# An encoder with eight experts: the whole down projection split, weights in 2 MB slabs, a short piece requested later

## The chip, the cores and the metric

The kernel runs on one core of a Trainium2 chip. Its time is the device time of one execution in microseconds (us); the times given are medians over runs on one chip. A profiled execution is one such run with the hardware profiler on.

## The reference, cut to what matters

Two batches of 256 tokens pass through two layers that share their weights. The change lies in the last block of the second layer, where each token goes through two of eight experts:

```python
def swiglu(x, w_g, w_u, w_d):
    return (jax.nn.silu(x @ w_g) * (x @ w_u)) @ w_d

def moe_swiglu(x, w_router, b_router, w_g, w_u, w_d):
    logits = (x @ w_router).astype(jnp.float32) + b_router.astype(jnp.float32)
    top_v, top_i = lax.top_k(logits, TOP_K)          # TOP_K = 2
    top_w = jax.nn.softmax(top_v, axis=-1)
    ...
    for e in range(N_EXPERTS):                        # 8
        y = y + combine[..., e:e + 1] * swiglu(x, w_g[e], w_u[e], w_d[e])
    return y
```

The width is 1024 (8 tiles of 128), an expert's hidden width 1408 (11 tiles). All is float32.

## The kernel before, in words

The attention, pooling, convolution and dense blocks run first and take until about 1040 us; the change does not touch their work. Then a router sorts the 512 tokens, twice each, into **items**: 128 rows that belong to one expert. Here there are 11 items. Their number is read from a table on the chip, so each engine's program has a first item (SP and VectorE), a loop, and a final item.

**Pieces.** The weights of an item come in 17 pieces (`PIECES`, line 74). Pieces 0 to 9 hold two feature blocks of gate and up weights, four of the eight contraction tiles each; piece 10 holds the last feature tile with all eight. Pieces 11, 12 and 13 are the first half of the output columns of the down projection, with contraction tiles 0 to 3, 4 to 7 and 8 to 10; pieces 14, 15 and 16 are the same for the second half. Pieces 13 and 16, with three contraction tiles, are the short ones: 128 partitions by 1536 numbers, where the others have 2048.

**Split products.** A float32 product is made from three fast ones: a matrix is split into a high part in the format fp32r and a low part, the rest. ScalarE writes the high part of a weight piece (`e_split`, lines 740 to 749), VectorE the low part (`e_low`, 1099 to 1105), and TensorE multiplies high by high, high by low and low by high (lines 1749 to 1751). The short pieces are not split: TensorE multiplies them as plain fp32 (line 1757), which the trace shows as two instructions per matmul. So the transposed hidden features are split for tiles 0 to 7 only (`hidden_high` 787, `hidden_low` 1215) and kept whole for tiles 8 to 10.

**Slots.** Fifteen pieces of an item pass through a ring of eight landing slots of 1 MB, six in `eraw` and two in `erawx`; the short pieces have two places of their own, `eplain`. Split parts lie in a ring of three (`ESPL`). SP requests the pieces in order (`expert_piece`, lines 469 to 483, waiting in `slot_free`, 485 to 502): a slot is free when VectorE has written the low part of what it held, a place of `eplain` when TensorE has used it. In the loop (515 to 523) SP requests pieces 3 to 16 of an item and then 0 to 2 of the next. A piece's rows are 2 KB long in memory, those of a short one 1.5 KB.

**The order of work** is written out by hand for each engine. TensorE (lines 1761 to 1780) takes pieces 0 to 16, transposes the hidden features of a block in between (1728), and turns the next item's rows into features behind piece 12 (1699). ScalarE (809 to 830) splits three pieces ahead of TensorE, with the tanh of each block, the high parts of the features, the load of the next item's rows behind piece 5's split (`load_rows`, 760), the next item's features (`xg_high`, 766 to 778) and the copies of the results (`y_out`, 795) in between. VectorE (1236 to 1254) follows with the low parts and the gating of the hidden rows; in the first item it also scales the residual (`residual_base`, 1193), in the last it adds gathered results into `X` (`add_rest`, 1268).

The lines that say how the last stretch of an item is ordered on ScalarE are:

```python
hidden_high(4, j)
e_split(14, j)            # the 15th split piece: piece 15
hidden_high(5, j)
e_split(0, j + 1)
xg_high(j + 1)
y_out(0, j)
e_split(1, j + 1)
e_split(2, j + 1)
y_out(1, j)
```

Of the kernel before, what the change touches and what calls it, by code (L numbers as in the profile page):

```python
# [34 lines left out]
P = 128  # L35
# [41 lines left out]
F_SPLIT = 8  # L77
SPLIT = [p for p in range(NPC) if p not in (13, 16)]
NSP = len(SPLIT)
RAWP = [p for p in range(NPC) if p not in SPLIT]  # L80
ERING, EMAIN, ESPL = 8, 6, 3
EW = 2048
N_BLK = 6
LOADS = [len([o for o in range(NSP) if o % ERING == s]) for s in range(ERING)]
# [3 lines left out]
C_COS, C_SIN, C_INV = 640, 896, 1152  # L88
C_I8, C_I16 = 1664, 1672
C_TOK = 1688  # L90
C_END = 1692
# [51 lines left out]
def build_trunk(nc, x0, x1, dense_w, expert_gu, expert_dn, consts, slots, vecs, mix, lnrow, wr, br, xd, yd, y0, y1):  # L143
    ctx = ExitStack()
    with ctx:
# [16 lines left out]

        cst = at("cst", [P, C_END], F32)
        vec = at("vec", [P, DEPTH, V_END], F32)
        hvec = at("hvec", [P, DEPTH, 32], F32)
        mixw = at("mixw", [P, DEPTH, 2, P], F32)
# [67 lines left out]
        eraw = at("eraw", [P, EMAIN, EW], F32)  # L234
# [10 lines left out]
        eplain = at("eplain", [P, 2, EW], F32, o)  # L245
        erawx = at("erawx", [P, ERING - EMAIN, EW], F32, o + 2 * EW * 4)
# [47 lines left out]
        hth = at("hth", [P, F_SPLIT, CAP], F32R)  # L294
        htl = at("htl", [P, F_SPLIT, CAP], F32R)
        ht32 = at("ht32", [P, FET - F_SPLIT, CAP], F32)
# [61 lines left out]
        in_plain = [sem(f"in_plain{i}") for i in range(2)]  # L358
# [26 lines left out]
        def landed(o, j):  # L385

            return j * (16 * LOADS[o % ERING]) + 16 * (o // ERING + 1)

        def raw_slot(o):

            s = o % ERING
            return eraw[:, s] if s < EMAIN else erawx[:, s - EMAIN]
# [45 lines left out]
        def _(sp):  # L438
# [30 lines left out]
            def expert_piece(e, p):  # L469
                what, b, k0, kn = PIECES[p]  # L470
                if what == "gu":
                    n = 2 * blk(b)
                    src = expert_gu[bass.ds(e * (2 * FET) + 4 * b, n), :, k0 * P:(k0 + kn) * P]
                else:
                    n = 4
                    src = expert_dn[bass.ds(e * KD + 4 * b, n), :, k0 * P:(k0 + kn) * P]
                if p in SPLIT:
                    o = SPLIT.index(p)
                    dst, arrived = raw_slot(o), in_e[o % ERING]
                else:  # L480
                    dst, arrived = eplain[:, RAWP.index(p)], in_plain[RAWP.index(p)]
                dst = dst[:, 0:n * kn * P].rearrange("p (c n) -> p c n", c=n)
                sp.dma_start(dst, src.rearrange("c p n -> p c n")).then_inc(arrived, 16)

            def slot_free(p, j, before=None):

                before = j - 1 if before is None else before
                if p not in SPLIT:
                    if isinstance(j, int) and j == 0:
                        sp.wait_ge(sel_mm, 2)  # L490
                    else:
                        sp.wait_ge(e_used, before * NPC + (p + 1))
                    return
                o = SPLIT.index(p)
                if o >= ERING:
                    sp.wait_ge(e_lo, j * NSP + (o - ERING + 1))
                elif isinstance(j, int) and j == 0:
                    if o >= EMAIN:
                        sp.wait_ge(sel_mm, 2)
                else:  # L500
                    last = max(q for q in range(NSP) if q % ERING == o)
                    sp.wait_ge(e_lo, before * NSP + (last + 1))

            for p in range(NPC):
                slot_free(p, 0)
                expert_piece(0, p)
                if p == EMAIN - 1:
# [4 lines left out]
            for p in range(ESPL):  # L512
                slot_free(p, 1)
                expert_piece(e, p)
            with sp.Fori(1, final) as j:

                e = sp.value_load(tab[0:1, bass.ds(j, 1)], min_val=0, max_val=NE - 1)
                for p in range(ESPL, NPC):
                    slot_free(p, j)
                    expert_piece(e, p)  # L520
                e = sp.value_load(tab[0:1, bass.ds(j + 1, 1)], min_val=0, max_val=NE - 1)
                for p in range(ESPL):
                    slot_free(p, j + 1)
                    expert_piece(e, p)
            e = sp.value_load(tab[0:1, bass.ds(final, 1)], min_val=0, max_val=NE - 1)
            before = sp.value_load(tab[0:1, 18:19], min_val=NE - 2, max_val=MAX_ITEMS - 2)
            for p in range(ESPL, NPC):
                slot_free(p, final, before)
                expert_piece(e, p)
# [14 lines left out]
        def _(act):  # L544
# [195 lines left out]
            def e_split(o, j):  # L740

                p = SPLIT[o]
                act.wait_ge(in_e[o % ERING], landed(o, j))
                if o >= ESPL:
                    act.wait_ge(e_used, j * NPC + (SPLIT[o - ESPL] + 1))
                elif not isinstance(j, int):
                    act.wait_ge(e_used, (j - 1) * NPC + (SPLIT[o - ESPL] + 1))
                n = (2 * blk(PIECES[p][1]) if PIECES[p][0] == "gu" else 4) * PIECES[p][3] * P
                nc.scalar.activation(ewhi[:, o % ESPL, 0:n], raw_slot(o)[:, 0:n], ACT.Copy).then_inc(e_hi, 1)  # L749
# [37 lines left out]
            def hidden_high(b, j):  # L787
# [3 lines left out]
                dst = hth[:, 2 * b:2 * b + n, :] if 2 * b < F_SPLIT else ht32[:, 2 * b - F_SPLIT:2 * b - F_SPLIT + n, :]  # L791
                nc.scalar.activation(dst, bank[B_HT[b % 2]][:, 0:n * CAP].rearrange("p (a n) -> p a n", a=n),
# [16 lines left out]
            with act.Fori(0, final) as j:  # L809
                for p in range(N_GUP):  # L810
                    if p % 2 == 1 or p == 10:
                        hidden_tanh(p // 2, j)
                    if p == 3:
# [5 lines left out]
                    e_split(p + ESPL, j)  # L819
# [11 lines left out]
            for p in range(N_GUP):  # L831
# [4 lines left out]
                e_split(p + ESPL, final)  # L836
# [9 lines left out]
            act.wait_ge(e_lo, final * NSP + ERING)  # L846
# [25 lines left out]
        def _(dve):  # L872
# [226 lines left out]
            def e_low(o, j):  # L1099

                p = SPLIT[o]
                n = (2 * blk(PIECES[p][1]) if PIECES[p][0] == "gu" else 4) * PIECES[p][3] * P
                dve.wait_ge(e_hi, j * NSP + (o + 1))
                V.tensor_tensor(ewlo[:, o % ESPL, 0:n], raw_slot(o)[:, 0:n], ewhi[:, o % ESPL, 0:n],  # L1104
                                ALU.subtract).then_inc(e_lo, 1)
# [109 lines left out]
            def hidden_low(b, j):  # L1215

                dve.wait_ge(ht_hi, j * N_BLK + (b + 1))
                V.tensor_tensor(htl[:, 2 * b:2 * b + 2, :],
                                bank[B_HT[b % 2]][:, 0:2 * CAP].rearrange("p (a n) -> p a n", a=2),
                                hth[:, 2 * b:2 * b + 2, :], ALU.subtract).then_inc(ht_lo, 1)  # L1220
# [15 lines left out]
            def item(j, first=False):  # L1236

                for p in range(N_GUP):
# [4 lines left out]
                    e_low(p + ESPL, j)  # L1243
# [33 lines left out]
            for p in range(N_GUP):  # L1277
# [4 lines left out]
                e_low(p + ESPL, final)  # L1282
                if p >= 5:
                    add_rest(p - 5)
            e_low(14, final)
            add_rest(6)
# [156 lines left out]
        def _(pe):  # L1443
# [269 lines left out]
            def item(j, more):  # L1713
# [7 lines left out]
                def hidden_features(b):  # L1721

                    pe.wait_ge(e_h, j * N_BLK + (b + 1))
                    if b >= 2:
                        pe.wait_ge(ht_hi, j * N_BLK + (b - 1))
                        pe.wait_ge(ht_lo, j * (F_SPLIT // 2) + (b - 1))
# [139 lines left out]
```

## Time and profile before

| what | value |
|---|---|
| median of 3 runs (lowest, highest) | 1646.91 us (1645.08, 1647.98) |
| profiled execution, its own time | 1647.25 us |
| its span | 1645.4 us |
| TensorE, VectorE, ScalarE, GpSimd busy | 1584.4, 1151.2, 807.4, 170.1 us |
| mean granted clock of TensorE | 0.988 of full speed |
| moved between memory and chip | 324.52 MB |

The span runs from the first to the last instruction of the profiled execution; 1.85 us of its time lie outside. A row of a timeline is one instruction (or a run of equal ones) with its start and duration. In the chain of waits every moment belongs to the one piece of work that the end waited for. "L749" is line 749. A matmul's busy time overlaps the next one's, since matmuls are pipelined; their pace is seen from start to start. Times on the axis count from the start of the span, so 1262 lies in the expert stage.

### The profile page before, as it was taken

Reading aid. Unit: us, or ns where it says so; the run is one execution under the profiler, and the core shown is the slowest. Engines: PE = TensorE matmul, PEld = TensorE weight load, DVE = VectorE, ACT = ScalarE, POOL = GpSimd, SP = SyncE. Lnnn points to the kernel's source line nnn. Section 1 sums busy time; section 2 is a strip of 40 time slices with the busy share of each in tenths; the row PEclk is TensorE's granted clock in tenths of the full one; section 3 lists DMA queues with packets and bytes.
Section 4 is the critical chain, followed back from the end, with each engine's and each line's share of the span. In section 5 each row is a group of like instructions: output and inputs, shape, how many; then the busy total and the mean of one; then the engine's idle time right before and its main releaser. Section 6 shows DMA issues by size and latency. Waiting matters only on the chain.

```text
span 1645.4 us, 20013 instructions
## 1 busy us (share of the span) xinstructions
PE 1584.4 (96%) x7315; PEld 1264.9 (77%) x7315; DVE 1151.2 (70%) x1339; ACT 807.4 (49%) x1095; POOL 170.1 (10%) x112
## 2 busy tenths in 40 slices
PE   7999999999999999999999999789999999999993
PEld 7877777888888888888777778567777777777772
DVE  6888846584434333288888574789888888888886
ACT  5344442252322222253444422557777777777763
POOL 0410005142000000004100051100000000000030
PEclk9999999999999999999999999899999999999997
DMA  5222222325454332212222235199999999999993
GB/s 211 77 91 76 77 102 90 103 76 202 145 201 144 102 122 96 101 66 77 100 67 77 77 115 206 64 397 392 384 372 381 370 371 372 375 372 381 375 337 142
DMA packets 133521, 324.52 MB, mean 197 GB/s; under 512 B 8188, under 2 KB 19836, under 8 KB 132944
## 3 DMA queue, kind: packets, MB, share of 16 engines
q1 hardware_dynamic: 124432, 290.27, 49.5%
q0 software_dynamic: 5872, 21.84, 3.5%
q10 hardware_dynamic: 3152, 11.54, 1.8%
q8 instruction: 42, 0.69, 0.2%
q14 instruction: 23, 0.19, 0.0%
HBM read 297.06 MB, written 27.26 MB: 197 GB/s over the span
## 4 chain that ended last, share of the span: by engine, by line
PE 91%; DVE 4%; issue 2%; ACT 1%; DMA 1%; POOL 1%; ACTq 0%; SPq 0%; DVEq 0%; POOLq 0%
PE bank L1464 15%; PE bank L1465 15%; PE bank L1466 15%; PE bank L1749 8%; PE bank L1751 8%; PE bank L1750 8%; PE bank L1503 4%; PE bank L1504 4%; PE bank L1502 4%; PE bank L1757 3%; PE bank L1728 1%; DVE ewlo L1104 1%; PE bank L1576 1%; PE bank L1589 1%; PE bank L1561 1%
## 5 line engine op out<-in xcount | busy, mean ns | idle before, releaser
L880 DVE TENSOR_TENSOR wlo<-raw,whi 128x1024 fp32r<-128x1024 f32 x170 | 238.9, 1408 | 207.7 <-ACT whi L554 207.4
L1464 PE MATMUL bank<-xth,whi 128*128 128x512 f32 (+1 forms) x976 | 381.5, 391 | 1.7 <-DVE wlo L880 1.7
L1465 PE MATMUL bank<-xtl,whi 128*128 128x512 f32 (+1 forms) x976 | 370.9, 380 | 0.0
L1466 PE MATMUL bank<-xth,wlo 128*128 128x512 f32 (+1 forms) x976 | 370.6, 380 | 0.0
L1104 DVE TENSOR_TENSOR ewlo<-eraw,ewhi 128x2048 fp32r<-128x2048 f32 x132 | 302.0, 2289 | 62.5 <-ACT ewhi L749 62.5
L749 ACT ACTIVATE ewhi<-eraw 128x2048 fp32r<-128x2048 f32 x132 | 252.2, 1911 | 42.8 <-PE bank L1751 42.8
L554 ACT ACTIVATE whi<-raw 128x1024 fp32r<-128x1024 f32 x170 | 178.5, 1051 | 137.0 <-PE bank L1504 123.9
L1464 PEld LDWEIGHTS bank<-xth,whi 128*128 128x128 f32 x976 | 184.3, 189 | 50.5 <-issue 8.5
L1465 PEld LDWEIGHTS bank<-xtl,whi 128*128 128x128 f32 x976 | 184.3, 189 | 36.8 <-issue 3.8
L1466 PEld LDWEIGHTS bank<-xth,wlo 128*128 128x128 f32 x976 | 184.1, 189 | 35.2
L1749 PE MATMUL bank<-ewhi,xgh 128*128 128x512 f32 (+1 forms) x528 | 205.9, 390 | 4.6 <-DVE xgl L1190 2.8
L1751 PE MATMUL bank<-ewhi,xgl 128*128 128x512 f32 (+1 forms) x528 | 197.7, 374 | 0.0
L1750 PE MATMUL bank<-ewlo,xgh 128*128 128x512 f32 (+1 forms) x528 | 197.2, 374 | 0.0
L1749 PEld LDWEIGHTS bank<-ewhi,xgh 128*128 128x128 f32 x528 | 100.2, 190 | 23.4 <-DVE ewlo L1104 4.3
L1750 PEld LDWEIGHTS bank<-ewlo,xgh 128*128 128x128 f32 x528 | 100.4, 190 | 18.7 <-issue 2.4
L1751 PEld LDWEIGHTS bank<-ewhi,xgl 128*128 128x128 f32 x528 | 100.0, 189 | 18.3
L614 ACT ACTIVATE gates<-bank,hvec 128x512 f32<-128x512 f32 x48 | 33.0, 688 | 126.2 <-PE bank L1466 126.2
L968 DVE SCALAR_TENSOR_TENSOR cv<-hpad,vec,cv 128x512 f32<-128x512 f32 x120 | 89.9, 750 | 3.1
L1104 DVE TENSOR_TENSOR ewlo<-erawx,ewhi 128x2048 fp32r<-128x2048 f32 x33 | 75.6, 2292 | 7.9 <-ACT ewhi L749 6.7
L1749 PE MATMUL bank<-ewhi,hth 128*128 128x512 f32 x176 | 75.5, 429 | 0.0
L749 ACT ACTIVATE ewhi<-erawx 128x2048 fp32r<-128x2048 f32 x33 | 63.2, 1916 | 16.2 <-PE bank L1751 14.2
L1751 PE MATMUL bank<-ewhi,htl 128*128 128x512 f32 x176 | 69.0, 392 | 0.0
(280 smaller groups left out, 2229.2 us busy)
## 6 DMA issues: line engine op xcount, KB each, us to landing
eraw<-expert_gu SPq DMA_DIRECT2D x99, 1024.0 KB, 8.2
raw<-dense_w SPq DMA_DIRECT2D x170, 512.0 KB, 3.5
eraw<-expert_dn SPq DMA_DIRECT2D x33, 1024.0 KB, 8.0
erawx<-expert_gu SPq DMA_DIRECT2D x22, 1024.0 KB, 8.2
eplain<-expert_dn SPq DMA_DIRECT2D x22, 768.0 KB, 10.1
erawx<-expert_dn SPq DMA_DIRECT2D x11, 1024.0 KB, 9.1
item_rows<-zero POOLq DMA_DIRECT2D x8, 1024.0 KB, 4.8
rows<-item_rows ACTq DMA_DIRECT2D x10, 512.0 KB, 7.1
```

The costliest lines, as they stand in the source:

```text
L554: nc.scalar.activation(whi[:, g % SPL, :], raw[:, g % RAW, :], ACT.Copy).then_inc(hi_done, 1)
L749: nc.scalar.activation(ewhi[:, o % ESPL, 0:n], raw_slot(o)[:, 0:n], ACT.Copy).then_inc(e_hi, 1)
L880: V.tensor_tensor(wlo[:, g % SPL, :], raw[:, g % RAW, :], whi[:, g % SPL, :], ALU.subtract).then_inc(lo_done, 1)
L968: ins = V.scalar_tensor_tensor(acc, src, w, acc, ALU.mult, ALU.add)
L1104: V.tensor_tensor(ewlo[:, o % ESPL, 0:n], raw_slot(o)[:, 0:n], ewhi[:, o % ESPL, 0:n], ALU.subtract).then_inc(e_lo, 1)
L1464: mm(out, wh, xh, start=first, stop=False)
L1465: mm(out, wh, xl, start=False, stop=False)
L1466: return mm(out, wl, xh, start=False, stop=last)
L1502: mm(out, ah[:, k, t], wh, start=(k == 0), stop=False)
L1749: mm(out, ah[:, k, :], wh, start=(k == 0), stop=False)
L1750: mm(out, ah[:, k, :], wl, start=False, stop=False)
L1751: ins = mm(out, al[:, k, :], wh, start=False, stop=(k == last - 1))
```

## The change

All eleven contraction tiles of the down projection are now split: pieces 13 and 16 get high and low parts like the others, in two places `eshi` and `eslo` of their own, and are multiplied with three fp32r matmuls per tile. The split features grow to eleven tiles. The ring has four slots of 2 MB: one request brings a slab of two pieces (pieces 0 and 1, 2 and 3, and so on; piece 10 alone; 11 and 12; 14 and 15) with rows of 4 KB, and a slot is free when the low parts of both its pieces are written. The two short pieces, called "a" and "b" in the list of requests, share one landing place, `eland`, which lies over constants that are no longer needed. "a" is requested between slabs 6 and 7; "b" once the low part of piece 13 is written, behind slabs 0 to 2 of the next item. The orders of ScalarE and VectorE follow, and the next item's rows are loaded behind piece 8's split.

The diff, cut to its core:

```diff
+SHORT = [13, 16]
+RING = [p for p in range(NPC) if p not in SHORT]
+ERING, EMAIN, ESPL = 4, 3, 3
+SLABS = [("gu", b, 4 if b < 5 else 2) for b in range(6)] + [("dn", h, 4) for h in range(2)]
+LOAD = [0, 1, 2, 3, 4, 5, 6, "a", 7]
+AHEAD = 3
...
+SLAB_END = [max(p for p in RING if slab_of(p) == i) for i in range(NSL)]
...
+        eland = at("eland", [P, 1536], F32, o_cst + 4 * C_COS)
...
+        eraw = at("eraw", [P, EMAIN, 2 * EW], F32)
...
-        eplain = at("eplain", [P, 2, EW], F32, o)
+        eshi = at("eshi", [P, 1536], F32R, o)
+        eslo = at("eslo", [P, 1536], F32R, o + EW * 4)
...
+            def slot_free(i, j, before=None):
...
+                if i == "a":
+                    if not isinstance(j, int):
+                        sp.wait_ge(e_lo, before * NPC + (SHORT[1] + 1))
+                elif i == "b":
+                    sp.wait_ge(e_lo, j * NPC + (SHORT[0] + 1))
+                elif i >= ERING:
+                    sp.wait_ge(e_lo, j * NPC + (SLAB_END[i - ERING] + 1))
...
+                    sp.wait_ge(e_lo, before * NPC + (SLAB_END[i - ERING] + 1))
...
             with sp.Fori(1, final) as j:
...
-                for p in range(ESPL, NPC):
-                    slot_free(p, j)
-                    expert_piece(e, p)
-                e = sp.value_load(tab[0:1, bass.ds(j + 1, 1)], min_val=0, max_val=NE - 1)
-                for p in range(ESPL):
-                    slot_free(p, j + 1)
-                    expert_piece(e, p)
+                following = sp.value_load(tab[0:1, bass.ds(j + 1, 1)], min_val=0, max_val=NE - 1)
+                for i in LOAD[AHEAD:]:
+                    slot_free(i, j)
+                    expert_load(e, i)
+                for i in LOAD[:AHEAD]:
+                    slot_free(i, j + 1)
+                    expert_load(following, i)
+                slot_free("b", j)
+                expert_load(e, "b")
...
-            for p in range(ESPL, NPC):
-                slot_free(p, final, before)
-                expert_piece(e, p)
+            for i in LOAD[AHEAD:] + ["b"]:
+                slot_free(i, final, before)
+                expert_load(e, i)
...
+                if p in SHORT:
+                    act.wait_ge(in_short, j * 32 + 16 * (SHORT.index(p) + 1))
+                    if p == SHORT[1]:
+                        act.wait_ge(e_used, j * NPC + (SHORT[0] + 1))
...
-                    if p == 3:
+                    if p == 6:
                         act.wait_ge(scattered, 16 * 2 * TT)
                         load_rows(j + 1)
...
                 e_split(14, j)
                 hidden_high(5, j)
+                e_split(15, j)
+                xg_high(j + 1)
+                e_split(16, j)
+                y_out(0, j)
                 e_split(0, j + 1)
-                xg_high(j + 1)
-                y_out(0, j)
                 e_split(1, j + 1)
...
+                hidden_low(4, j)
                 e_low(14, j)
+                hidden_low(5, j)
                 if first:
                     for i in range(5, 8):
                         residual_base(i)
                     last_slots()
+                e_low(15, j)
+                xg_low(j + 1)
+                e_low(16, j)
                 e_low(0, j + 1)
-                xg_low(j + 1)
...
-                pe.wait_ge(ht_hi, j * N_BLK + 6)
+                pe.wait_ge(ht_lo, j * N_BLK + 6)
                 piece(13)
```

In the new code `e_split(p)` and `e_low(p)` count pieces; before they counted split pieces only, so that `e_split(14)` was piece 15.

## Rows read from the trace of the kernel before

**Rows 1.** Stretches, 1260 to 1310: us, engines' busy us, clock, DMA share, GB/s

```profile
1260.00:1310.00 50.00, 50.00 (x228) 39.02 (x227) 41.28 (x35) 37.53 (x41) 0.00 (x0) 1.00 1.02 370
```

**Rows 2.** Chain of waits, 1250 to 1350: start us, us, engine, line

```profile
by line: PE bank L1751 28.2%; PE bank L1749 28.1%; PE bank L1750 28.1%; PE bank L1757 10.3%; PE bank L1728 3.6%; PE bank L1699 1.7%
...
1262.19 2.58 PE bank L1757 x6
...
1310.45 0.87 PE bank L1699 x8
1311.32 2.58 PE bank L1757 x6
1314.13 0.23 PE bank L1750
...
1319.35 2.58 PE bank L1757 x6
```

**Rows 3.** Waits, all engines 1060 to 1646, then SP's own 1100 to 1600

```profile
ACT ewhi L749 <- PE bank L1751: 57.0, 43, 6.5
...
SPq L483 <- DVE ewlo L1104: 365.7, 138, 5.8
```

**Rows 4.** Stretches, while the first 1 MB pieces land

```profile
1015.00:1020.00 5.00, 5.00 (x24) 4.14 (x23) 4.97 (x9) 0.62 (x2) 0.00 (x0) 1.00 1.05 387
```

**Rows 5.** Groups by line, 1030 to 1646: busy us, mean ns, idle before

```profile
L1104 DVE TENSOR_TENSOR ewlo<-eraw,ewhi 128x2048 fp32r<-128x2048 f32 x132 | 302.0, 2289 | 62.5 <-ACT ewhi L749 62.5
L749 ACT ACTIVATE ewhi<-eraw 128x2048 fp32r<-128x2048 f32 x132 | 252.2, 1911 | 42.8 <-PE bank L1751 42.8
...
L1218 DVE TENSOR_TENSOR htl<-bank,hth 128x256 fp32r<-128x256 f32 x44 | 18.4, 418 | 0.0
```

**Rows 6.** Timeline of VectorE, end of item 0: start us, us

```profile
1120.79 2.29 DVE L1104 TENSOR_TENSOR ewlo<-eraw,ewhi 128x2048 fp32r<-128x2048 f32 x1
1122.99 1.29 DVE L1190 TENSOR_TENSOR xgl<-xg,xgh 128x512 fp32r<-128x512 f32 x2
```

**Rows 7.** Chain of waits, end of item 0

```profile
1122.84 2.58 PE bank L1757 x6
```

**Rows 8.** Chain of waits, end of the last item

```profile
1612.37 1.29 DVE X L1274
1613.68 1.30 DVE X L1274
1615.00 2.61 DMA item_rows<-X
```

**Rows 9.** DMA, 6 to 16 us, where loads have 4 KB rows

```profile
DMA packets 1293, 4.12 MB, mean 412 GB/s; under 512 B 205, under 2 KB 333, under 8 KB 1293
```

**Rows 10.** DMA requests, 400 to 700: KB each, median us to landing

```profile
raw<-dense_w SPq DMA_DIRECT2D x55, 512.0 KB, 3.5
```

**Rows 11.** Timeline of VectorE, item 4: start us, us, line

```profile
1283.47 2.29 DVE L1104 TENSOR_TENSOR ewlo<-eraw,ewhi 128x2048 fp32r<-128x2048 f32 x1 [0.31 <-ACT ewhi L749]
...
1295.21 2.29 DVE L1104 TENSOR_TENSOR ewlo<-eraw,ewhi 128x2048 fp32r<-128x2048 f32 x1 [0.29 <-ACT ewhi L749]
```

**Rows 12.** Timeline of ScalarE, item 4

```profile
1290.12 1.91 ACT L749 ACTIVATE ewhi<-eraw 128x2048 fp32r<-128x2048 f32 x1
...
1293.26 1.91 ACT L749 ACTIVATE ewhi<-eraw 128x2048 fp32r<-128x2048 f32 x1
...
1316.42 0.58 ACT L800 ACTIVATE yrows<-bank 128x512 f32<-128x512 f32 x1
```

**Rows 13.** Stretches around gaps of TensorE (column three is its busy time)

```profile
339.00:342.00 3.00, 0.61 (x5) 0.37 (x4) 2.19 (x7) 2.97 (x7) 0.00 (x0) 0.98 0.00 0
342.00:345.30 3.30, 3.30 (x17) 3.30 (x17) 3.20 (x11) 3.16 (x8) 0.00 (x0) 0.50 0.02 5
...
1593.00:1595.20 2.20, 0.19 (x2) 0.06 (x1) 2.17 (x5) 0.00 (x0) 1.54 (x2) 1.00 1.05 374
```

More of the change, by code:

```diff
@@ L76, with slab_of @@
 NPC = len(PIECES)
[L77 to L81, printed above, removed]
+SHORT = [13, 16]
+RING = [p for p in range(NPC) if p not in SHORT]
+ERING, EMAIN, ESPL = 4, 3, 3
 EW = 2048
 N_BLK = 6
-LOADS = [len([o for o in range(NSP) if o % ERING == s]) for s in range(ERING)]
+SLABS = [("gu", b, 4 if b < 5 else 2) for b in range(6)] + [("dn", h, 4) for h in range(2)]
+NSL = len(SLABS)
+LOAD = [0, 1, 2, 3, 4, 5, 6, "a", 7]
+AHEAD = 3
+def slab_of(p):
+    what, b, k0, kn = PIECES[p]
+    return b if what == "gu" else 6 + b
+SLAB_END = [max(p for p in RING if slab_of(p) == i) for i in range(NSL)]
 C_ID, C_BLK, C_MEAN, C_ONE, C_TRI = 0, 128, 256, 384, 512
[L88 to L91, printed above, removed]
+C_I8, C_I16 = 640, 648
+C_COS, C_SIN, C_INV = 672, 928, 1184
+C_TOK = 664
+C_END = 1696
 SKIP = 4096
@@ L357, in build_trunk @@
         in_e = [sem(f"in_e{i}") for i in range(ERING)]
-        in_plain = [sem(f"in_plain{i}") for i in range(2)]
+        in_short = sem("in_short")
         e_hi, e_lo, e_used = sem("e_hi"), sem("e_lo"), sem("e_used")
@@ L383, in quarters, with landed, slab, piece_of_slab @@
             return ap.rearrange("p (c n) -> p c n", c=4)
[L385 to L392, printed above, removed]
+        def landed(i, j):
+            return j * (16 * NSL // ERING) + 16 * (i // ERING + 1)
+        def slab(i):
+            s, n = i % ERING, SLABS[i][2]
+            t = eraw[:, s] if s < EMAIN else erawx[:, s - EMAIN]
+            return t[:, 0:n * D].rearrange("p (c n) -> p c n", c=n)
+        def piece_of_slab(p):
+            k0, kn = PIECES[p][2:]
+            if p in SHORT:
+                return by_column(eland, p)
+            return slab(slab_of(p))[:, :, k0 * P:(k0 + kn) * P]
+        def parts(p):
+            if p in SHORT:
+                return by_column(eshi, p), by_column(eslo, p)
+            o = RING.index(p) % ESPL
+            return by_column(ewhi[:, o], p), by_column(ewlo[:, o], p)
+        def by_column(t, p):
+            n, kn = SLABS[slab_of(p)][2], PIECES[p][3]
+            return t[:, 0:n * kn * P].rearrange("p (c n) -> p c n", c=n)
         def blk(b):
@@ L467, in _, with expert_load @@
             sp.wait_ge(mg_lo, 2 * KD)
-            def expert_piece(e, p):
-                what, b, k0, kn = PIECES[p]
+            def expert_load(e, i):
+                if i in ("a", "b"):
+                    h = "ab".index(i)
+                    what, b, n, k0, kn = "dn", h, 4, KD, FET - KD
+                    dst = by_column(eland, SHORT[h])
+                    arrived = in_short
+                else:
+                    what, b, n = SLABS[i]
+                    k0, kn, dst, arrived = 0, KD, slab(i), in_e[i % ERING]
@@ L497, in slot_free @@
                 elif isinstance(j, int) and j == 0:
-                    if o >= EMAIN:
+                    if i >= EMAIN:
                         sp.wait_ge(sel_mm, 2)
                 else:
[L501 to L507, printed above, removed]
+                    sp.wait_ge(e_lo, before * NPC + (SLAB_END[i - ERING] + 1))
@@ L508, in _ @@
+            for i in LOAD:
+                slot_free(i, 0)
+                expert_load(0, i)
+                if i == EMAIN - 1:
                     sp.dma_start(slot_no[:, :], slots).then_inc(in_slots, 16)
@@ L1097, in x_low, with e_low @@
                 V.tensor_tensor(xrl[:, tt, :], X[:, tt, :], xrh[:, tt, :], ALU.subtract).then_inc(xr_lo, 1)
[L1099 to L1105, printed above, removed]
+            def e_low(p, j):
+                hi, lo = parts(p)
+                dve.wait_ge(e_hi, j * NPC + (p + 1))
+                V.tensor_tensor(lo, piece_of_slab(p), hi, ALU.subtract).then_inc(e_lo, 1)
             for tt in range(TT):
@@ L1281, in _ @@
                     hidden_low(p // 2 - 1, final)
-                e_low(p + ESPL, final)
+                e_low(p + 3, final)
                 if p >= 5:
                     add_rest(p - 5)
+            hidden_low(4, final)
             e_low(14, final)
+            hidden_low(5, final)
+            e_low(15, final)
+            e_low(16, final)
             add_rest(6)
```

110 lines of the change are left out of this document (43 added, 67 removed).

## The prediction

> **What bounds the kernel now.** I read the stretches first: over 50 us of the expert stage TensorE is busy for all 50.00 and the DMA engines are full (share 1.02), so there are two candidates; VectorE is busy for 41.28, ScalarE for 37.53 [rows 1]. The chain of waits decides between them: over two items it consists of TensorE lines alone, and the fp32 matmuls of the short piece 13 start at 1262.19 and at 1311.32, so one item lasts 49.13 us [rows 2]. The waits add that ScalarE's split (L749) waits for TensorE and not for a landing, and that SP waits for VectorE's low parts, which free the slots [rows 3]. So TensorE is the bound, and the weights come early enough. They move at 387 GB/s when the queue is full [rows 4], while an item moves 17.3 MB of weights (three matrices of 1024 by 1408) and 1 MB of rows, 373 GB/s over 49.13 us. Transfers have little to spare, and their order matters.
>
> **The matmuls.** A short piece is six fp32 passes, 2.58 us; afterwards it is nine fp32r matmuls of 0.23 us, 2.07 us [rows 2]. That is 0.51 us off the path per piece, 22 pieces, 11.2 us, if nothing else is late.
>
> **Splitting the short pieces.** ScalarE gets two more splits per item. A 2048-column one takes 1.911 us, a 1536-column one three quarters of it, 1.43; VectorE's low part takes 2.289, so 1.72 [rows 5]. With two more low parts of the transposed features (0.418 each at two tiles, about 0.29 for the single last tile [rows 5]) VectorE gets 4.15 us more per item. Inside the loop the 8.7 us it has free in 50 cover that. ScalarE's 2.9 us fit as well. In the first and last item VectorE has no such cover. In item 0 it also scales the residual: the low part of the next item's piece 0 ran from 1120.79 to 1123.08, the two low parts of the rows behind it [rows 6]. Now 1.72 + 0.42 + 0.29 + 1.29 + 1.72 = 5.44 us come before it, so it ends at 1128.5, where TensorE was ready at 1122.84 + 2.58 = 1125.4 [rows 7]: **3.1 us**. In the last item the chain runs over VectorE's last two additions into X and the store behind them, not over TensorE [rows 8], and all of the 4.15 us stand ahead: **4.1 us**. The bounds of these two are 0, if VectorE could start so much earlier, and 5.4 and 4.2. Piece 13 also waits now for the last low part of the features, which stands behind piece 14's on VectorE; by the rows' times it is done at about 1311.4, when TensorE comes to piece 13 at 1311.32 [rows 2]: nothing to 0.1.
>
> **The slabs.** 2 MB in 4 KB rows replace pairs of 1 MB in 2 KB rows. The nearest rows with 4 KB rows, at the kernel's start, move 412 GB/s [rows 9], so a slab takes 5.09 us where two pieces took 5.42. I take 412, as it has the row length itself; 387 is the other end. A short piece keeps its 1.5 KB rows: 0.79 MB, 2.03 us at 387 (1.91 at 412). The load of the next item's rows, 0.5 MB on ScalarE's queue, takes 1.27 us; it moves from behind piece 5's split to behind piece 8's, at 1292.0, and is used at 1310.45 [rows 2, 12]; nobody waits for that. From request to landing without a queue, a 512 KB load takes 3.5 us [rows 10], of which 1.27 is data: 2.2 us of delay.
>
> **The later request.** This is the term that decides. SP asks for the second short piece ("b", piece 16) behind the next item's slabs 0, 1 and 2, and not before the low part of piece 13, since both share one landing place. Behind b on SP stand only next item's slab 3 and onward, which wait for piece 15 anyway; behind b's split on ScalarE, however, stand the copy of the result and the splits of the next pieces 0 to 2, and behind its low part those pieces' low parts. I follow the requests in the item that ran to 1321.9. The low part of piece 5, which frees slab 6's slot, ends at 1283.47 + 2.29 = 1285.76 [rows 11]. Add 2.2, then in order of the queue slab 6 (5.09), the first short piece (2.03), the rows (1.27), slab 7, slabs 0, 1 and 2 of the next item (4 x 5.09) and b (2.03): b lands at 1318.7. Each slab in between is asked for before its predecessor has landed (slab 0's slot is free at 1295.21 + 2.29 = 1297.5 [rows 11]), so the queue doesn't run dry. Before, TensorE began piece 16 at 1319.35 [rows 2]; with 0.51 saved in piece 13 it would be 1318.84. But b still needs 1.43 + 1.72 us: 1321.9, **3.1 us late**. It would have to land by 1315.6. The chain goes on: after b's split come the copy, 0.58 [rows 12], the split of piece 0, 1.91, and its low part, 2.29, until 1325.0, where TensorE used to begin piece 0 at 1319.35 + 2.58 = 1321.93. With 0.2 for the hand-overs, an estimate from piece 9, whose split ended at 1295.17 and whose low part began at 1295.21 [rows 11, 12], an item gets 3.3 us longer. Ends: 1.6 if the queue ahead of slab 0 were empty (1297.5 + 2.2 + 3 x 5.09 + 2.03 = 1317.0, 1.7 earlier), 5.0 if slabs go at 387. This holds for items 1 to 9, **9 x 3.3 = 29.7 us**. Item 0 has its 3.1 already, with VectorE reaching b's low part only at about 1124, and in the last item no slabs stand ahead of b. SP's nine requests per item in place of 17 and the new places of the constants cost nothing: SP only waits, and the constants are loaded once.
>
> For the transfers the Trainium skill (DMA: Bandwidth & Descriptors, Anatomy of one DMA) gives about 2.0 us fixed and 436 GB/s. An estimate by that page: b lands 2.1 us earlier, an item gets 1.2 us longer, the sum is 1665 us. Rows 9 and 10 show 412 GB/s and 2.2 us instead, so I keep these.
>
> **The clock.** The gap of 3 us is new for TensorE in this stage. Its granted clock fell to 1.2 GHz for at least 3.3 us after a gap of 2.4 us between 339 and 342, and stayed at 2.4 GHz through a gap of 2.0 between 1593 and 1595.2 [rows 13]. The new gap is nearer to the first, though light work surrounded that. 3.3 us at half clock cost up to 1.65; part falls into the gap before piece 0, which waits for VectorE anyway. Between 0 and 0.8 I take 0.5 per item: **4.5 us**. The Trainium skill (TensorE: Matmul & The Clock Gate, HAM oscillation) describes such a fall at every tile where a wait for data recurs; by it the term is nearer 0.8, the sum 1691.
>
> **Sum.** 3.1 + 4.1 + 29.7 + 4.5 = 41.4 us. The matmuls' saving is contained in the late starts. The profiled execution took 1647.25 us, 1.85 outside its span of 1645.4 and 0.34 over the median of the runs: 1647.25 + 41.4 - 0.34 = 1688.3.
>
> **Rivals.** *TensorE stays the bound everywhere*: the 11.2 us are kept, 1636. For it speaks that TensorE has no gap now; it needs b landed by 1315.6, 3.1 us sooner than the sum gives, and both outer items free of VectorE. Chance 0.05. *b is in time, but VectorE eats the gain at both ends*: 9 x 1.0 saved against 7.2, 1645. This is where the change does too little to measure. 0.05. *Partly late*: the queue ahead of slab 0 is empty, 1.6 us per item and a gap too short for the clock: 14.4 + 7.2, 1668.5. The full DMA engines [rows 1] speak against it. 0.14. (The page's 1665 lies beside this.) *4 KB rows bring nothing* and slabs go at 387: 1.7 more per item, 1704. The 412 speaks against it. 0.06. My forecast, with 1684 to 1692 by its clock term alone, has 0.70.
>
> **Numbers.** No change means within 0.2%, what a measurement of this kernel can tell. The range takes in the forecast, the partly late case with the outer items at their bound of 0 (1661), and the slow slabs with the outer items' upper bounds and 0.8 for the clock (1709); left out are the first two rivals and a little beyond. The chances by sign are those of the cases: faster 0.05, same 0.05, slower 0.90.
>
> **What would show it.** ScalarE's split waiting for the landing of the short piece, once per item in items 1 to 9; a TensorE gap of about 3 us ahead of piece 16 and a smaller one ahead of piece 0; a period near 52.5; idle DMA engines early in an item instead of none; 4 KB packets at about 412 GB/s; the fp32 line gone, and a clock under 1.00 in the stage. I am wrong if b lands before 1.43 + 1.72 us ahead of its need, or if the period is under 49.

## The result, and the profile after

The changed kernel takes 1702.36 us (median of 4 runs, 1697.79 to 1705.03), the kernel before, measured beside it, 1646.41: ratio 1.0335, 95% interval 1.032 to 1.035. It is slower, and the time lies in the range, 14 us above the forecast. The profiled execution has a span of 1703.2 us, 57.8 more than before. The following rows answer to those shown ahead of the prediction.

The stretches of the changed kernel (columns as in [rows 1]):

```profile
1260.00:1310.00 50.00, 46.25 (x209) 37.56 (x209) 39.97 (x33) 36.00 (x39) 0.00 (x0) 0.93 0.85 328
...
1510.00:1560.00 50.00, 46.85 (x221) 37.93 (x220) 40.33 (x36) 34.85 (x40) 0.00 (x0) 0.99 0.92 355
```

TensorE has lost 3.75 of its 50.00 us [rows 1], its mean clock is 0.93 instead of 1.00, and the DMA engines, which were full, are so no longer (0.85). No engine is busier than before: the item waits for something that begins late. The chain of waits from 1250 to 1350 names it (start us, us, engine or DMA, line):

```profile
by line: DMA eland<-expert_dn 21.0%; PE bank L1792 17.4%; PE bank L1794 16.4%; PE bank L1793 16.4%; issue 8.8%; DVE eslo L1144 7.1%; ACT ewhi L787 3.8%; ACT eshi L787 3.0%; PE bank L1776 2.4%; DVE ewlo L1144 1.7%; DVE eb L1248 1.4%; DVE eh 
...
1327.88 10.45 DMA eland<-expert_dn
1338.42 1.49 ACT eshi L787
1339.94 1.77 DVE eslo L1144
1341.75 0.79 PE bank L1792
```

Where TensorE stood alone [rows 2], the second short piece b now leads: asked for at 1327.88, landed 10.45 us later, split, subtracted, and only then multiplied. The waits from 1060 to 1700 (us in total, times, longest) say the same for the whole stage:

```profile
ACT eshi L787 <- DMA eland<-expert_dn: 43.5, 10, 6.3
...
PE bank L1792 <- DVE eslo L1144: 32.5, 9, 3.8
```

ScalarE's split of b waits for the landing in item 0 (1.5 us), in items 1 to 9 and in the last one; the view counts ten of these, as it puts item 4's down to TensorE, though b landed only 0.10 us before that wait ended. Nine times, in items 1 to 9, TensorE stands still for it, 3.6 us on average. Why b takes 10.45 us is seen in the requests (SyncE's timeline, first number the start; x3 is three requests from 1316.87 on) and in the transfers from 1310 to 1335:

```profile
1316.87 9.19 SPq L516 DMA_DIRECT2D eraw<-expert_gu  x3
1327.88 0.37 SPq L516 DMA_DIRECT2D eland<-expert_dn  x1
```

```profile
DMA packets 2930, 10.30 MB, mean 412 GB/s; under 512 B 96, under 2 KB 608, under 8 KB 2930
```

b stands behind slabs 0, 1 and 2 of the next item, 6 MB at 412 GB/s, the rate of [rows 9]. What follows the gap is the second part of the loss, seen in TensorE's timeline (the bracket is its idle time and what ended it) and in the stretches of piece 16 and of the 2.65 us behind it:

```profile
1341.75 0.79 PE L1792 MATMUL bank<-eshi,hth 128*128 128x512 f32 x1 [3.42 <-DVE eslo L1144]
```

```profile
1341.75:1345.75 4.00, 4.00 (x9) 3.14 (x10) 3.53 (x2) 4.00 (x3) 0.00 (x0) 0.50 0.23 92
1345.75:1348.40 2.65, 2.65 (x10) 2.13 (x9) 2.65 (x2) 0.63 (x2) 0.00 (x0) 0.70 0.32 93
```

The nine matmuls of piece 16 take 4.00 us at half clock, where nine at 0.23 take 2.07. A mean clock of 0.70 over the next 2.65 us means that 1.6 of them were at half clock too.

To compare all kernels, the trace's first gate matmul of each item gives three lengths. "Middle" is the mean of items 1 to 9; "last" runs to the end of the span:

| kernel | starts at | item 0 | middle | last | median us |
|---|---|---|---|---|---|
| before | 1066.9 | 57.97 | 49.12 | 78.4 | 1646.4 |
| after | 1068.1 | 59.15 | 54.47 | 85.8 | 1702.4 |
| e1 b before slab 2 | 1068.0 | 58.85 | 48.43 | 86.3 | 1650.3 |
| e2 half slabs | 1067.9 | 59.58 | 55.42 | 85.0 | 1712.0 |
| e3 gap filled | 1068.0 | 62.10 | 53.02 | 85.0 | 1692.7 |
| e4 slabs only | 1066.6 | 56.67 | 49.08 | 79.5 | 1647.4 |
| e5 additions first | 1068.0 | 59.14 | 54.52 | 83.9 | 1701.9 |
| e6 e1 + additions earlier | 1066.3 | 59.12 | 48.41 | 86.5 | 1649.5 |
| e7 e6 + residual spread | 1065.2 | 52.51 | 48.79 | 86.6 | 1647.6 |
| e8 b first | 1065.6 | 58.82 | 51.35 | 88.1 | 1677.0 |
| e9 e7 + features' low part earlier | 1065.5 | 52.29 | 48.42 | 84.0 | 1639.4 |
| e10 e6 + the same, last item | 1065.7 | 58.83 | 48.40 | 83.1 | 1647.4 |
| e11 before + residual spread | 1069.6 | 53.23 | 49.08 | 78.9 | 1643.1 |

Of the 57.8 us, 9 x 5.35 = 48.1 come from the middle items, 7.3 from the last, 1.2 from item 0, and 1.2 from the start of the stage, which differs by up to 4.4 us from one kernel's profile to another's (e7 and e11), so that the 1.2 can't be laid to the change.

### The profile page after: what moved, and what is told of

Same layout as the page of the kernel before. It is cut to its first block, busy times and chain, and to the rows that moved or that the text cites. A ratio compares the mean times of both kernels' runs of the same rounds, so it can differ in the third digit from the quotient of the medians.

```text
span 1703.2 us, 19901 instructions
## 1 busy us (share of the span) xinstructions
PE 1599.3 (94%) x7381; PEld 1291.4 (76%) x7381; DVE 1192.4 (70%) x1383; ACT 835.7 (49%) x1117; POOL 169.5 (10%) x112
## 4 chain that ended last, share of the span: by engine, by line
PE 79%; DMA 7%; DVE 7%; issue 3%; ACT 3%; POOL 0%; SPq 0%; ACTq 0%; DVEq 0%; POOLq 0%
PE bank L1512 15%; PE bank L1513 14%; PE bank L1514 14%; PE bank L1792 6%; DMA eland<-expert_dn 6%; PE bank L1793 6%; PE bank L1794 6%; PE bank L1550 4%; PE bank L1552 4%; PE bank L1551 4%; DVE eslo L1144 2%; ACT ewhi L787 1%; DVE ewlo L1144 1%; PE bank L1624 1%; PE bank L1637 1%
## 5 line engine op out<-in xcount | busy, mean ns | idle before, releaser
L1144 DVE TENSOR_TENSOR ewlo<-eraw,ewhi 128x2048 fp32r<-128x2048 f32 x121 | 275.2, 2289 | 35.8 <-ACT ewhi L787 35.8
L787 ACT ACTIVATE ewhi<-eraw 128x2048 fp32r<-128x2048 f32 x121 | 229.0, 1909 | 32.6 <-PE bank L1794 32.6
L1144 DVE TENSOR_TENSOR ewlo<-erawx,ewhi 128x2048 fp32r<-128x2048 f32 x44 | 100.5, 2285 | 2.4 <-ACT ewhi L787 2.4
L787 ACT ACTIVATE ewhi<-erawx 128x2048 fp32r<-128x2048 f32 x44 | 84.3, 1916 | 0.0
L1144 DVE TENSOR_TENSOR eslo<-eland,eshi 128x1536 fp32r<-128x1536 f32 x22 | 38.6, 1754 | 50.2 <-ACT eshi L787 50.2
L1792 PE MATMUL bank<-ewhi,hth 128*128 128x512 f32 x176 | 71.7, 408 | 1.6 <-DVE ewlo L1144 1.6
## 6 DMA issues: line engine op xcount, KB each, us to landing
erawx<-expert_dn SPq DMA_DIRECT2D x11, 2048.0 KB, 10.3
```

What stands on the lines that cost most here:

```text
L787: nc.scalar.activation(parts(p)[0], piece_of_slab(p), ACT.Copy).then_inc(e_hi, 1)
L1144: V.tensor_tensor(lo, piece_of_slab(p), hi, ALU.subtract).then_inc(e_lo, 1)
L1792: mm(out, ah[:, k, :], hi[:, :, cols], start=(k == 0), stop=False)
```

## The experiments

**1. Only the place of b's request.** In item 0 and in the loop b goes ahead of slab 2; everything else is the changed kernel.

```diff
-                for i in LOAD[:AHEAD]:
+                for i in LOAD[:2]:
                     slot_free(i, j + 1)
                     expert_load(following, i)
                 slot_free("b", j)
                 expert_load(e, "b")
+                slot_free(2, j + 1)
+                expert_load(following, 2)
```

> The second short piece is requested between the next item's slabs 1 and 2 instead of behind slab 2; nothing else differs from the changed kernel. Theory (its late landing behind three slabs of the next item is what stalls TensorE): it lands some 5.1 us earlier, about 1333.4 in the item that was looked at, against 1336.8 needed for no gap, so the gap of 3.4 us ahead of its piece and the fall of the clock go from items 1 to 9; the item period comes to 48.5 to 49.3 us instead of 54.6, and the time to 1650 us (1645 to 1657). The gain at the last item isn't there, since the order of its own requests is as it was. Rival (the added splitting on ScalarE and VectorE, or the 2 MB slabs in four places, holds TensorE back): the gap moves to another piece and the time stays above 1690.

Measured: 1650.28 us, ratio to before 1.0016 (1.0006 to 1.0026); 52 us of the loss are gone with the order of two requests. Its stretch, SyncE's requests and TensorE's start of piece 16 (no idle time ahead of it, so no bracket):

```profile
1260.00:1310.00 50.00, 49.76 (x240) 40.59 (x239) 46.02 (x38) 40.55 (x42) 0.00 (x0) 1.00 0.98 380
```

```profile
1308.22 0.37 SPq L516 DMA_DIRECT2D eland<-expert_dn  x1
1308.85 0.37 SPq L516 DMA_DIRECT2D eraw<-expert_gu  x1
```

```profile
1318.52 0.39 PE L1796 MATMUL bank<-eshi,hth 128*128 128x512 f32 x1
```

The clock is 1.00 throughout this stretch, the middle item 48.43 us, 0.69 *shorter* than before. So the added splits cost little inside the loop: of the 1.0 us per item that the fp32r matmuls can save, 0.69 arrive (9 x 0.69 = 6.2 us), and TensorE waits 0.2 us ahead of piece 13, for the last low part of the features. It is given back: 7.9 us in the last item, 0.9 in item 0.

**2. The rate of the queue.** Each slab is requested as two halves of 1 MB with 2 KB rows, in the same order.

```diff
-            return j * (16 * NSL // ERING) + 16 * (i // ERING + 1)
+            return j * (32 * NSL // ERING) + 32 * (i // ERING + 1)
...
+                for half in ([0, 4] if i not in ("a", "b") else [None]):
+                    if half is not None:
+                        k0, kn, dst = half, 4, slab(i)[:, :, half * P:(half + 4) * P]
```

> Each slab is requested as two halves of 1 MB with 2 KB rows into the same place; order and waits stay those of the changed kernel. Theory (the second short piece lands late because five slabs stand in the queue between the low part of piece 5 and it, so the period is the queue's time plus the rest of that loop): each slab takes 5.42 us (2.1 MB at the 387 GB/s that the kernel before showed with 2 KB rows) instead of 5.12, five of them 1.5 us more, the period 56.1 us, the time 1702 + 9 x 1.5 = 1716 us (1710 to 1722). Rival (the short piece is late because of its request, held by the low part of piece 13, not because of the queue's rate): no change, 1700 to 1705.

Measured: 1712.02 us. Transfers from 1310 to 1335, and b in the chain of waits:

```profile
DMA packets 4951, 9.81 MB, mean 392 GB/s; under 512 B 161, under 2 KB 673, under 8 KB 4951
```

```profile
1328.70 12.20 DMA eland<-expert_dn
```

With 392 instead of 412 GB/s b takes 12.2 instead of 10.45 us to land, and the middle item grows by 0.95 us. The queue ahead of b sets the period; large requests with 4 KB rows are worth some 10 us here, where b is late (row length and number of requests were changed together). The size falls short of the expected 13.5 for two reasons. The rate did not fall to 387: from the end of piece 5's low part to b's landing an item takes 34.8 us on average, in the changed kernel 33.5, and 1.3 is what five slabs at 392 add. And in four of the nine items the clock was low for only half as long.

**3. The clock.** Work that nobody reads fills the gap.

```diff
                 piece(15)
+                if more:
+                    for _ in range(14):
+                        mm(bank[2][:, :], hth[:, 0, :], hth[:, 0:4, :], start=True, stop=True)
                 piece(16)
```

> Fourteen more matmuls of 128 x 512 with results that nobody reads go between pieces 15 and 16 of every item but the last (3.2 us at 0.23 each, in a gap of 3.4). Theory (TensorE's clock falls for 6.8 us once per item because of the gap, and this adds 1.2 to 1.7 us to the loop that sets the period, as pieces 16 and 0 run at half speed): the clock stays at 1.00, the seven items with a fall get 1.2 to 1.7 us shorter, the time comes to 1688 to 1695 us. Rival (the loop is set by the queue and the splits alone and the slow matmuls are caught up elsewhere): no change, 1700 to 1705.

Measured: 1692.67 us. Its stretch:

```profile
1260.00:1310.00 50.00, 48.96 (x232) 39.50 (x231) 41.71 (x36) 37.03 (x40) 0.00 (x0) 1.00 0.89 342
```

The clock stays at 1.00, and a middle item takes 53.02 instead of 54.47 us: 1.45 us of each item is the slow clock alone, since b comes as late as before (from piece 5's low part to its landing 33.6 us on average, 33.5 in the changed kernel). (In item 0, which has no such gap, the added matmuls cost 3 us.) The remaining 53.02 - 49.12 = 3.9 us is the stall, less what the matmuls save; against experiment 1, where b is in time, it is 4.6.

**4. The slabs without the split.** Four slots of 2 MB, but contraction tiles 8 to 10 in plain fp32 again, in two places that are refilled as soon as TensorE has used them.

```diff
-LOAD = [0, 1, 2, 3, 4, 5, 6, "a", 7]
+LOAD = [0, 1, 2, 3, 4, 5, 6, "a", 7, "b"]
...
-        eshi = at("eshi", [P, 1536], F32R, o)
-        eslo = at("eslo", [P, 1536], F32R, o + EW * 4)
+        eplain = at("eplain", [P, 2, EW], F32, o)
```

> The slabs of 2 MB in four places alone: contraction tiles 8 to 10 are again multiplied in plain fp32 from two places of their own, which are requested in the old order (the second one behind the second slab of the down projection, with no wait for the first one's low part). Theory (the stall comes from the place shared by the short pieces and the late request): there is no stall ahead of piece 16, TensorE stays the bound and the period is that of the kernel before, 49.3 us; the time is 1646 us (1641 to 1652). Rival (four large places instead of eight small ones free too late and starve the splits): 1665 us or more.

Measured: 1647.41 us, ratio 0.9998 (0.9988 to 1.0007): no change. The chain from 1250 to 1350 is TensorE alone again, with the fp32 matmuls of piece 13 49.08 us apart:

```profile
1260.46 2.58 PE bank L1795 x6
...
1309.54 2.58 PE bank L1795 x6
```

The coarser ring starves nobody, and faster transfers are worth nothing where TensorE is the bound.

**5. b first.** The other way round: b ahead of slab 0.

```diff
+                slot_free("b", j)
+                expert_load(e, "b")
                 for i in LOAD[:AHEAD]:
                     slot_free(i, j + 1)
                     expert_load(following, i)
-                slot_free("b", j)
-                expert_load(e, "b")
```

> The changed kernel with the second short piece requested ahead of the next item's slab 0. Theory (one issuer, in order: whatever stands first and waits, holds the rest): the short piece is in time, but slab 0 can't be requested before the low part of piece 13 is done, lands 9.3 us after that and is split 4.3 us later, so piece 0 comes some 1.3 us late per item: period 49.7 us, 1662 us in all (1655 to 1672), between the changed kernel and the order of the first experiment. Rival (the earlier the request the better): 1650 us or less.

Measured: 1677.0 us. SyncE asks for slab 0 right behind b at 1265.63, once piece 13's low part is done, and ScalarE waits for it and then for slab 1:

```profile
1265.00 0.37 SPq L516 DMA_DIRECT2D eland<-expert_dn  x1
1265.63 1.81 SPq L516 DMA_DIRECT2D eraw<-expert_gu  x3
```

```profile
1274.73 3.71 ACT L787 ACTIVATE ewhi<-eraw 128x2048 fp32r<-128x2048 f32 x2 [1.57 <-DMA eraw<-expert_gu]
1279.84 1.93 ACT L787 ACTIVATE ewhi<-eraw 128x2048 fp32r<-128x2048 f32 x1 [1.40 <-DMA eraw<-expert_gu]
```

The wait is the expected one; its size, 2.9 us per item over experiment 1, is twice the expected 1.3. ScalarE waits for slab 1 too, and TensorE then stands twice, ahead of piece 0 and behind piece 2:

```profile
1279.02 0.50 PE L1792 MATMUL bank<-ewhi,xgh 128*128 128x512 f32 x1 [1.50 <-DVE ewlo L1144]
...
1288.38 0.44 PE L1776 MATMUL bank<-cst,eh 128*128 128x128 f32 x2 [0.90 <-DVE eh L1252]
```

Two places too early cost less (26.7 us over experiment 1) than one too late (52.1), but b's wait holds all that stands behind it.

**6. The last item.** In the changed kernel the chain there runs from b's landing over its two splits to the last additions ("issue", 1.64, is VectorE's low part of b: its timeline has it at 1668.85, for 1.76):

```profile
1659.76 7.47 DMA eland<-expert_dn
...
1667.34 1.50 ACT eshi L787
...
1668.89 1.64 issue
1670.53 1.29 DVE X L1318
...
1671.84 1.30 DVE X L1318
1673.16 2.62 DMA item_rows<-X
```

Experiment e5 moves the two additions ahead of b's low part there, nothing else:

```diff
             e_low(15, final)
-            e_low(16, final)
             add_rest(6)
             add_rest(7)
+            e_low(16, final)
```

> The changed kernel with one move: in the last item VectorE makes the last two additions (rests 6 and 7) ahead of the low part of the second short piece instead of behind it. Theory (that low part waits 3.1 us for its landing with the additions queued behind it, and the end of the kernel hangs on the last addition and the transfer behind it): the additions end about 4.9 us earlier; then ScalarE's first normalisation, which begins 4.2 us after its own split of the short piece, ends next, so 2.9 us is what the end gains: 1699.5 us (1698 to 1701). Rival (the end hangs on TensorE's last piece or on ScalarE's passes): no change, 1702.

Measured: 1701.86 us, a miss: no change that 4 runs can show. The last item is 1.9 us shorter in the profile, where 2.9 was expected; its chain still leads from b's landing over ScalarE, whose passes over the outputs (L896) stand behind the split of b. The same was tried on experiment 1's order, with the additions further ahead:

```diff
             e_low(14, final)
+            add_rest(6)
+            add_rest(7)
             hidden_low(5, final)
             e_low(15, final)
             e_low(16, final)
-            add_rest(6)
-            add_rest(7)
```

> The order with the short piece between the next item's slabs 1 and 2, and in the last item the last two additions right behind the low part of piece 14 (their rows have landed by 1603.5 and 1607.7, that low part ends at 1608.9). Theory: the last item loses 2.9 us against the order alone, until ScalarE's first normalisation ends next: 1650.3 - 2.9 = 1647.4 us (1646 to 1648.5), the same as the kernel before within its measurement. Rival: no change against 1650.3.

Measured: 1649.47 us, a miss again. What holds ScalarE then, from 1600 to 1616:

```profile
ACT eshi L791 <- PE bank L1798: 9.3, 1, 9.3
```

Not b's landing but TensorE: the high parts of both short pieces share one place, and piece 13 still used it. Piece 13 was late because it needs the last block of hidden features, whose 0.28 us low part e6 puts behind 4.8 us of other VectorE work (2.28 and twice 1.28). Experiment e10 puts that low part first:

```diff
             hidden_low(4, final)
+            hidden_low(5, final)
             e_low(14, final)
             add_rest(6)
             add_rest(7)
-            hidden_low(5, final)
```

> The kernel with the short piece between slabs 1 and 2 and the two additions behind the low part of piece 14, with the one move in the last item alone: the last block's low part ahead of that of piece 14. Theory: piece 13 starts some 3 us earlier there, ScalarE splits the second short piece when it has landed (about 1611) instead of at 1614.2, the end comes 2.8 us earlier: 1646.7 us (1645.5 to 1648). Rival: no change against 1649.5.

Measured: 1647.38 us, ratio to before 1.0004 (0.9996 to 1.0013); the last item falls from 86.5 to 83.1 us, and ScalarE's wait is for the landing again:

```profile
1609.92 1.49 ACT L791 ACTIVATE eshi<-eland 128x1536 fp32r<-128x1536 f32 x1 [6.00 <-DMA eland<-expert_dn]
```

**7. The residual steps spread out.** VectorE's eight residual steps all lie in item 0, where the change leaves VectorE no room. Experiment e7 shares them out, on top of e6:

```diff
-                    if first and p >= 6:
-                        residual_base(p - 6)
+                    if bases and p == 10:
+                        residual_base(bases[0])
...
                 e_low(15, j)
+                if bases:
+                    residual_base(bases[1])
...
-            item(0, True)
-            with dve.Fori(1, final) as j:
+            item(0, True, (0, 1))
+            for n in (1, 2, 3):
+                item(n, False, (2 * n, 2 * n + 1))
+            with dve.Fori(4, final) as j:
```

> As the run before it, and the eight residual steps of VectorE (1.28 us each) that all lie in item 0 are shared out, two each in items 0 to 3. Theory (with the splits of the short pieces VectorE has no room for them in item 0, which lasts 10.4 us longer than an item in the middle, 2.5 of it at the low clock, but has 2 to 3 us free in every other item): item 0 gets 5 to 7 us shorter, items 1 to 3 up to 1.3 us longer each: 1642.5 us (1640 to 1646), under the kernel before. Rival (item 0 is long because of its loads and the clock): no gain, 1647 us or more.

Measured: 1647.55 us, a miss by the median. Item 0 falls as expected, from 59.12 to 52.51 us, but items 1 to 3 take 49.57 each, 1.2 more. TensorE's timeline in item 2, ahead of piece 13, shows the features' low part again:

```profile
1207.17 0.49 PE L1798 MATMUL bank<-eshi,hth 128*128 128x512 f32 x1 [1.51 <-DVE htl L1262]
```

So e9 puts that low part ahead of piece 14's in every item, as e10 does in the last.

> The spread residual steps and the short piece between slabs 1 and 2, and now the low part of the last block of hidden features (0.28 us) stands ahead of the low part of piece 14 (2.28 us) in every item; the last two additions stay behind the low part of piece 14. Theory (in items 0 to 3 TensorE waits 1.5 us ahead of piece 13 for that block, and in the last item piece 13 comes late for it, holds the place of the short pieces' high part, and with it ScalarE's split of the second one and ScalarE's passes over the outputs): items 1 to 3 get 1.1 us shorter each, item 0 1.4, the last 2.8, so 1647.5 - 7.5 = 1640 us (1638 to 1643), under the kernel before by 0.4%. Rival (those waits are made up later in the item): 1645 us or more.

Measured: 1639.41 us (1639.14 to 1641.53), ratio to before 0.9964 (0.9951 to 0.9977). Items 1 to 3 are back at 48.4. The spread has nothing to do with the change, so it was also given to the kernel before:

> The kernel before with its residual steps shared out over items 0 to 3 in the same way, nothing of the change in it: what the spread is worth without the change. Theory (item 0 there is 8.9 us longer than a middle item, 2.5 of it by the low clock; VectorE has 8 us free in every other item): item 0 gets 4 to 6 us shorter and items 1 to 3 stay, 1642.5 us (1640 to 1645). Then the best version of the change may gain 2 to 3 us over it at most. Rival (item 0 is long there because of its loads): 1647 us.

Measured: 1643.07 us, ratio 0.9977 (0.9968 to 0.9986). Of e9's 7.3 us (the kernel before took 1646.71 beside it) the spread alone explains 3.6. The other 3.7, between the two medians, would be the gain that the change could have brought, with b in time and a better order on VectorE, against the 11.2 us of its matmuls. But by the lengths in the table e9's expert stage is only 1.8 us shorter than e11's: 9 x 0.66 = 5.9 and 0.9 gained in the loop and in item 0, 5.1 lost in the last item. The rest lies ahead of the stage, which begins at 1065.5 and 1069.6 in these two profiles, so a gain of about 2 to 4 us is what the runs support.

## Why the prediction was right, and where its sizes were off

The time lies in the range partly by luck. The clock, the stall and the last item each cost more than forecast, and the clock and the last item more than the upper bounds given for them. What made room for that was the slow slabs in the range, 9 x 1.7 us, which did not come: they moved at 412 GB/s. Without this room the range would have ended near 1693.

**The later request** decided, as the prediction put it: b lands behind three slabs, ScalarE waits for it once per item, TensorE stands still ahead of piece 16. Experiments 1 and 5 show that the request's place alone makes it, experiment 2 that the queue's rate sizes it, experiment 4 that the slabs as such cost nothing. The stall, less the matmuls' saving, measured 3.9 us per item (experiment 3); the prediction had 3.3, counted in the same way. Its working can be followed in item 4. From the end of piece 5's low part (1305.03) to b's landing (1338.32) it took 33.3 us, against 1318.7 - 1285.76 = 32.9 forecast; from the landing to piece 16 3.43 against 3.15, as each hand-over between engines takes 0.04 to 0.1 and the two operations 1.49 and 1.76.

**The clock** is the term that was mis-sized most: 0.5 us per item forecast, 1.45 measured, and 0.8 was given as its bound. The prediction counted 3.3 us at half clock. The stretches of piece 16 have 4.00 + 1.6 = 5.6, which cost 2.8 us of matmul time. It was right that part of this falls into a gap ahead of piece 0, but the gap is small. It is seen in item 8, where the clock stayed at full (first row: TensorE is busy for 3.51 of 4.00 us); the second row is item 9:

```profile
1560.76:1564.76 4.00, 3.51 (x14) 2.61 (x15) 3.53 (x2) 4.00 (x4) 0.00 (x0) 1.00 0.17 69
1613.82:1617.82 4.00, 4.00 (x11) 3.19 (x12) 3.53 (x2) 4.00 (x4) 0.00 (x0) 0.60 0.21 78
```

The clock fell behind eight of the nine waits, for a shorter time in item 9, and not behind item 8's, although that one lasted 3.70 us and item 4's 3.42; why is not shown. The rule of the Trainium skill (TensorE: Matmul & The Clock Gate, HAM oscillation), a fall at every tile where a wait for data recurs, was nearer than my 0.5. Together the stall and the clock gave 48.1 us where 34.2 stood.

**Item 0**: 3.1 us forecast, 1.2 measured, and not at the place that was forecast. VectorE's added work makes TensorE stand ahead of pieces 13 and 15 there, not ahead of the next item's piece 0; for the wait ahead of piece 13 the prediction had nothing to 0.1:

```profile
1115.45 0.49 PE L1792 MATMUL bank<-eshi,hth 128*128 128x512 f32 x1 [1.77 <-DVE htl L1258]
...
1122.13 0.50 PE L1792 MATMUL bank<-ewhi,hth 128*128 128x512 f32 x1 [1.63 <-DVE ewlo L1144]
```

A saving was overlooked as well. I wrote of the moved load of the next rows that nobody waits for it. But the load itself waits for the scatter of the rows into memory, and before the change ScalarE stood there for 2.86 us: the load went out at 1083.67, and the split of piece 6, queued behind it, began at 1084.15. The low part of piece 6 on VectorE and then the piece on TensorE, before, and the same low part after:

```profile
1086.10 2.29 DVE L1104 TENSOR_TENSOR ewlo<-erawx,ewhi 128x2048 fp32r<-128x2048 f32 x1 [2.66 <-ACT ewhi L749]
...
1088.45 0.50 PE L1749 MATMUL bank<-ewhi,xgh 128*128 128x512 f32 x1 [1.76 <-DVE ewlo L1104]
```

```profile
1084.88 2.28 DVE L1144 TENSOR_TENSOR ewlo<-erawx,ewhi 128x2048 fp32r<-128x2048 f32 x1
```

With the later place VectorE's 2.66 us and TensorE's 1.76 us of waiting are gone. Experiment 4 has the move without the split, and its item 0 is 1.3 us shorter than before. That a moved step's own wait was the cause is read from these rows; the move was not tried alone.

**The last item**: 4.1 us forecast, 7.3 measured. The chain still ends over the last additions and the store, but what they wait for is b's landing, which the prediction did not have there. I took VectorE's added work, but wrote that no slabs stand ahead of b and left it there; b's request waits for piece 13's low part in this item too, and VectorE stood 3.1 us for its landing with the last additions behind it. In e10, with the additions ahead of this wait and the block of features in time, the last item is still 4.7 us longer than before. That is close to the 4.1, but e10's chain still leads from b's landing over ScalarE's split to ScalarE's passes, so the nearness does not show that VectorE's work is what is left.

**The slabs** at 412 GB/s and **the matmuls** were right: 0.69 us less per middle item in experiment 1, of the 1.0 that 2 x 0.51 allows. The figures of the Trainium skill that the prediction set beside its rows (DMA: Bandwidth & Descriptors, Anatomy of one DMA) are fitted there to transfers that GpSimd issues, while SyncE issues these; by the estimate from them an item would have become 1.2 us longer, where the stall alone measured 3.9. SyncE has ten requests per item, not nine, which changed nothing. The rival of *a gain eaten at both ends* (1645) is what experiment 1 turned into, once b was in time: 1650.3. *4 KB rows bring nothing* fell with 412 GB/s, *partly late* with 3.9 us of stall.

## What to carry to other kernels

A queue that one engine issues in order is a schedule: when a request gets a new wait or a later place, add up all the bytes that will stand between it and its use, and do the same for what then stands behind it. Work that saves time in the loop can cost it in the first and last iteration, where the engine that gets it has other duties; a 0.3 us operation put behind 4.8 us of other work there held two other engines (e6). And a gap on TensorE can cost more than its length: here 3.4 to 3.8 us of waiting cost about another 1.5 in slow matmuls.

## What was not expected of the hardware

Fourteen matmuls with unread results made the kernel 10 us faster (experiment 3), by holding the clock at 1.00 through the same wait. And in the last item, while the gathers of the results run beside it, one 2 MB slab took 15.43 us from its request to its landing (1636.57 to 1652.00), where the median of the eleven requests for this slab, one per item, is 10.3, as the profile's list of requests has it (that the gathers slowed it was not tested):

```profile
erawx<-expert_dn SPq DMA_DIRECT2D x11, 2048.0 KB, 10.3
```
